# A product of constants ahead of each attention step's transposes in a one-core decoder kernel

## The chip, the cores and the metric

The kernel runs on one core of a Trainium2 chip. The metric is the device time of one execution, in microseconds (us). A profiled execution has a span (first to last instruction) that is a little shorter than its time.

## What is computed

The reference is one inference step of a decoder trunk of two layers, for a prompt of 512 tokens and for 8 sample tokens with the same weights. Layer 0 has differential attention heads and mLSTM heads side by side, layer 1 is a gated linear recurrence, and each layer ends in a SwiGLU channel mixer. Everything is float32. The part that matters here is the prompt attention of layer 0, for 4 heads and 4 blocks of 128 queries:

```python
s = jnp.einsum('bqhjd,bshjd->bhjqs', q_blk, kf)      # two key maps, j = 0, 1
s = s - slopes * dist.astype(jnp.float32)
s = jnp.where(dist >= 0, s, -jnp.inf)
p = jax.nn.softmax(s, axis=-1)
w = p[:, :, 0] - lam * p[:, :, 1]
return jnp.einsum('bhqs,bshv->bqhv', w, vf)
```

## The kernel before

The program is a setup, the input projection of layer 0, a "middle" (attention, mLSTM, the sample tokens' attention over the cached pages, and what is left of the adaLN modulation), then the output projection and the large matrix products of the rest. The order on every engine is written out by hand; engines meet only through semaphores.

The middle (`middle_pe` for TensorE) is a loop of 18 steps (s from 0 to 17), fully unrolled. Each step works on one attention unit (head h = s // 4, query block s % 4) at several stages of its life. On TensorE (PE) step s issues, in this order:

- `head_sums` (L2515 to L2527), in steps 4, 8, 12 and 16; `head_scores(s)` (L2501), the mLSTM scores; `pv(s-2)` (L2558), attention weights times values; `head_rows` (L2491) in every fourth step
- `block_products` (L2921): 64 small products for one block of the modulation, until the blocks run out
- `scores(s+1)` (L2539): the attention scores of the next unit
- `transposes(s-1)` (L2548): the weights of unit s-1, one to four tiles of 128x128, in steps 1 to 16, so 16 calls and 40 transposes in all
- `block_turn` (L2937): one product that turns the block of the step before
- then, by step: `query_rows` (L2567, steps 0 to 5), the sample tokens' work (L2577 to L2638) and `square_sums` (L2651)

PSUM is used as a ring of four buffers of two banks (`ps(g)`, group g in buffer g % 4). Every use has a number fixed by `plan()`. `begin(g)` lets PE wait until the use four before it was released by the engine that reads it, and `done` announces the result. So `head_scores(s+1)` begins only when VectorE has released the scores of `scores(s+1)`, which stand four places before it.

VectorE (DVE) issues in each step: `biased(s)` (L1591: reads and releases the scores), `past_products` for a sample token (L1640, L1644) in steps 0 to 6, `maxima` (L1597), `weights(s-1)` (L1605 to L1610, the last of which writes `Wb` and raises `w_ready`), `decayed(s)` (L1622), `block_rows` (L2046: copies `block_products`' result), `block_select` (L2060: reads `block_turn`'s result), `past_sums` (L1649, L1650), and further sample work in steps 7 to 12. Each of its calls waits for the one before it. ScalarE (ACT) takes exponentials, and `unit_wT` (L1016) copies the transposes' result out of PSUM. GpSimd (POOL) loads the cache pages (L725), two for each sample token, when the page buffer was read.

`transposes(u)` writes only the first bank of its group, and `unit_wT` reads only that one:

```python
g = use[("T", u)]
begin(g)
pe.wait_ge(w_ready, u + 1)
for kb in range(u % 4 + 1):
    ins = T.transpose(ps(g)[:, 0, kb * P:(kb + 1) * P], Wb[u % 2][:, kb * P:(kb + 1) * P], ident)
done(ins)
```

`ident` and the columns from `C_SEL` are both parts of the tile `cn`, which is loaded once with constants.

Of the kernel before, what the change touches and what calls it, by code (L numbers as in the profile page):

```python
# [69 lines left out]
C_ID, C_ADA, C_MASK, C_DIST, C_SEL, C_COMB, C_SLOPE, C_DROW = 0, 128, 168, 296, 808, 1832, 1896, 1897  # L70
# [158 lines left out]
def trunk(nc, a, o):  # L229
# [34 lines left out]
    with ExitStack() as ctx:  # L264
        def sb(name, shape, dt=F32):
            return ctx.enter_context(nc.sbuf_tensor(name, shape, dt))
# [11 lines left out]
        cn = sb("cn", [P, C_END])  # L278
# [21 lines left out]
        ident = cn[:, C_ID:C_ID + P]  # L300
# [177 lines left out]
        def ps(g):  # L478
            return psum[g % NGRP]
# [1960 lines left out]
        def middle_pe(pe, begin, done, block_products, block_turn):  # L2440
            T = nc.tensor
# [9 lines left out]
            for tb in range(4):  # L2451
                g = use[("kv", tb)]
# [9 lines left out]
            for key, first in (("stokA", 0), ("stokB", 8)):  # L2462
                g = use[key]
# [4 lines left out]
            for tb in range(4):  # L2468
                g = use[("bkv", tb)]
# [7 lines left out]
            g = use["acol"]  # L2477
# [4 lines left out]
            g = use["gs"]  # L2482
# [60 lines left out]
            def transposes(u):  # L2543
                g = use[("T", u)]
                begin(g)
                pe.wait_ge(w_ready, u + 1)
                for kb in range(u % 4 + 1):
                    ins = T.transpose(ps(g)[:, 0, kb * P:(kb + 1) * P], Wb[u % 2][:, kb * P:(kb + 1) * P], ident)  # L2548
                done(ins)
# [115 lines left out]
            for s_ in range(STEPS):  # L2665
# [14 lines left out]
                if 1 <= s_ < 17:  # L2680
                    transposes(s_ - 1)
# [23 lines left out]
            for i, t in enumerate(MIXED):  # L2705
                g = use[("rb", t)]
# [3 lines left out]
                if t == "S":  # L2710
                    for u in range(8):
                        h, j = u % 4, u // 4
                        ins = T.matmul(ps(g)[:, 0, 8 * u:8 * u + 8], cn[:, C_SEL + j * P:C_SEL + (j + 1) * P], R4[:, h, P:P + 8],
                                       start=True, stop=True)
# [3 lines left out]
                for q in range(4):  # L2718
                    b = 2 * q + j
                    ins = T.matmul(ps(g)[:, q // 2, (q % 2) * P:(q % 2 + 1) * P], cn[:, C_SEL + b * P:C_SEL + (b + 1) * P], R4[:, h, 0:P],  # L2720
                                   start=True, stop=True)
# [324 lines left out]
```

## Time and profile before

| | us |
|---|---|
| median of 3 runs | 1548.38 |
| lowest and highest | 1545.55 and 1753.03 |
| the profiled execution: time | 1548.51 |
| the profiled execution: span | 1546.9 |
| PE busy | 1419.4 (92%) |
| DVE busy | 785.6 (51%) |
| ACT busy | 532.5 (34%) |
| mean granted clock of PE | 0.955 |

The clock is given as a share of full speed: 1.0 is 2.4 GHz and 0.5 is 1.2 GHz. A float32 product shows as more than one MATMUL record (a 512-column product as two), a transpose as one. Busy shares are means over stages of different kinds. Times of single instructions are read from the timeline, where a row's start and the start of the next row tell what the first one costs in a row of work.

### The profile page before, as it was taken

How to read it: one execution, taken by the hardware profiler on the slowest of the kernel's cores; microseconds unless marked ns; L12 is line 12 of the kernel's file. 1: busy time of each engine (PE TensorE's matmuls, PEld its weight loads, DVE VectorE, ACT ScalarE, POOL GpSimd, SP SyncE). 2: the span in 40 equal slices, each digit the busy share in tenths (PEclk: the TensorE clock that was granted, in tenths of full speed). 3: DMA queues.
4: the chain of work that ended last, by engine and by line, in shares of the span. 5: the costliest groups of instructions: out<-in, count | busy, mean ns of one | idle time of the engine just before them, and what ended most of it. 6: DMA issues, size and time to landing. Idle time of an engine off the chain costs nothing.

```text
span 1546.9 us, 29445 instructions
## 1 busy us (share of the span) xinstructions
PE 1419.4 (92%) x12244; PEld 1354.5 (88%) x12244; DVE 785.6 (51%) x1181; ACT 532.5 (34%) x759; POOL 321.6 (21%) x303
## 2 busy tenths in 40 slices
PE   4999967879797999999999989988989999999996
PEld 4899956656597999999999979987989999999995
DVE  4523256763466633333324679887574333333356
ACT  1211142332423333112222346884433321222224
POOL 2000031111116500000001626534543000000054
PEclk8999988978898999999999999998999999999998
DMA  9632287756632132243322402211613224422211
GB/s 320 197 98 56 83 292 268 236 188 205 209 109 83 55 82 67 83 113 107 86 71 76 137 23 87 96 52 54 167 32 109 65 58 115 129 84 65 75 38 56
DMA packets 213504, 175.07 MB, mean 113 GB/s; under 512 B 9079, under 2 KB 183932, under 8 KB 213252
## 3 DMA queue, kind: packets, MB, share of 16 engines
q1 hardware_dynamic: 208448, 160.13, 33.7%
q0 software_dynamic: 4800, 13.23, 2.7%
q8 instruction: 81, 1.33, 0.4%
q14 instruction: 35, 0.29, 0.1%
q10 hardware_dynamic: 140, 0.09, 0.0%
HBM read 167.87 MB, written 5.63 MB: 112 GB/s over the span
## 4 chain that ended last, share of the span: by engine, by line
PE 53%; DVE 11%; ACT 3%; issue 2%; POOL 0%; DVEq 0%; ACTq 0%; POOLq 0%
PE ps L2747 44%; PE ps L2776 4%; PE ps L2756 4%; DVE gn L2196 2%; DVE wlo L1982 1%; DVE UL L2203 1%; DVE xc L2314 1%; ACT whi L1173 1%; DVE rstd L2169 1%; DVE tv L2161 0%; DVE xc L2349 0%; ACT xT L1247 0%; DVE xc L2348 0%; DVE xT L2146 0%; DVE xT L2164 0%
## 5 line engine op out<-in xcount | busy, mean ns | idle before, releaser
L2747 PE MATMUL ps<-UH,whi 128*128 128x260 f32 x1840 | 371.5, 283 | 11.2 <-DVE wlo L1982 10.8
L2747 PE MATMUL ps<-UH,wlo 128*128 128x260 f32 x1840 | 371.4, 284 | 0.0
L2747 PE MATMUL ps<-UL,whi 128*128 128x260 f32 x1840 | 370.8, 283 | 0.0
L1173 ACT ACTIVATE whi<-raw 128x2048 fp32r<-128x2048 f32 (+3 forms) x104 | 178.0, 1712 | 440.8 <-PE ps L2747 388.3
L2747 PEld LDWEIGHTS ps<-UH,whi 128*128 128x128 f32 x1840 | 284.2, 189 | 13.0 <-DVE wlo L1982 9.7
L2747 PEld LDWEIGHTS ps<-UH,wlo 128*128 128x128 f32 x1840 | 284.4, 189 | 0.0
L2747 PEld LDWEIGHTS ps<-UL,whi 128*128 128x128 f32 x1840 | 283.4, 189 | 0.0
L1982 DVE TENSOR_TENSOR wlo<-raw,whi 128x2048 fp32r<-128x2048 f32 (+3 forms) x104 | 224.1, 2155 | 77.8 <-ACT whi L1173 77.2
L2250 DVE TENSOR_TENSOR hb<-ps,silb 128x520 f32<-128x520 f32 x44 | 30.8, 699 | 268.0 <-PE ps L2747 247.9
L825 POOL COPY accS<-xT 128x520 f32<-128x520 f32 x4 | 2.5, 626 | 620.0 <-DVE xT L2128 620.0
L2747 PE MATMUL ps<-HH,whi 128*128 128x260 f32 x484 | 97.4, 283 | 0.0
L2747 PE MATMUL ps<-HH,wlo 128*128 128x260 f32 x484 | 97.1, 282 | 0.0
L2747 PE MATMUL ps<-HL,whi 128*128 128x260 f32 x484 | 97.1, 282 | 0.0
L2747 PEld LDWEIGHTS ps<-HH,whi 128*128 128x128 f32 x484 | 74.6, 189 | 0.0
L2747 PEld LDWEIGHTS ps<-HL,whi 128*128 128x128 f32 x484 | 74.5, 188 | 0.0
L2747 PEld LDWEIGHTS ps<-HH,wlo 128*128 128x128 f32 x484 | 74.2, 188 | 0.0
L2125 DVE TENSOR_TENSOR stmp<-ps,modT 128x8 f32<-128x8 f32 x36 | 6.0, 167 | 133.1 <-PE ps L2747 116.8
L2921 PE MATMUL ps<-raw,cF 128*32 128x128 f32 x1536 | 57.9, 314 | 16.5 <-DMA raw<-in_w_ada 10.1
L2921 PEld LDWEIGHTS ps<-raw,cF 128*32 128x32 f32 x1536 | 49.2, 128 | 25.7 <-DMA raw<-in_w_ada 8.5
L1320 ACT ACTIVATE silb<-ps 128x520 f32<-128x520 f32 x44 | 26.7, 606 | 127.1 <-PE ps L2747 109.3
L857 POOL TENSOR_TENSOR xT<-xT,mu 128x256 f32<-128x256 f32 x64 | 47.5, 743 | 50.9 <-ACT mu L1221 46.5
L725 POOL DMA_DIRECT2D page<-in_cache_k x16 | 8.9, 559 | 213.7 <-PE ps L2455 181.4
(509 smaller groups left out, 2577.0 us busy)
## 6 DMA issues: line engine op xcount, KB each, us to landing
raw<-in_w_ada SPq DMA_DIRECT2D x96, 512.0 KB, 6.2
raw<-in_w_ffn_in SPq DMA_DIRECT2D x88, 512.0 KB, 5.0
raw<-in_w_in_even SPq DMA_DIRECT2D x24, 512.0 KB, 4.7
raw<-in_w_ffn_out SPq DMA_DIRECT2D x32, 384.0 KB, 4.0
raw<-in_w_ffn_out SPq DMA_DIRECT2D x32, 320.0 KB, 3.4
raw<-in_w_in_odd SPq DMA_DIRECT2D x20, 512.0 KB, 4.6
raw<-in_w_out_odd SPq DMA_DIRECT2D x16, 320.0 KB, 3.6
page<-in_cache_k POOLq DMA_DIRECT2D x16, 256.0 KB, 4.5
```

What stands on the lines that cost most here:

```text
L857: pool.tensor_tensor(x, x, mu[:, hf, 0:HALF], ALU.subtract).then_inc(d_ready, 1)
L1173: ins = nc.scalar.activation(whi[w % 2][:, 0:f], raw[c % NRAW][:, 0:f], ACT.Identity)
L1320: ins = nc.scalar.activation(silb[c % 2][:], pT(g), ACT.Silu)
L1982: ins = v.tensor_tensor(wl_[:, 0:f], raw[c % NRAW][:, 0:f], wh[:, 0:f].bitcast(F32), ALU.subtract)
L2169: v.reciprocal(rstd[:, hf], tv[:, hf]).then_inc(rstd_ready, 1)
L2196: v.scalar_tensor_tensor(gn[:, t], xT[:, t, hf, 0:HALF], gain, rstd[:, hf, 0:HALF], ALU.mult, ALU.mult).then_inc(n_ready, 1)
L2203: v.scalar_tensor_tensor(UL[:, t, hf, 0:HALF], gn[:, t], B9[:, r + 1, t, 0:1], UH[:, t, hf, 0:HALF].bitcast(F32), ALU.add, ALU.subtract).t ...
L2250: v.tensor_tensor(hb[c % 2][:], pT(g), silb[c % 2][:], ALU.mult).then_inc(h_ready, 1)
L2747: ins = T.matmul(ps(g)[:, hf, 0:HT], wt(k, m), x[:, k, hf], start=(k == 0 and wt is wh and x is xh), stop=(k == s.k - 1 and wt is wl_))
L2756: ins = T.matmul(ps(g)[:, hf, 0:HT], wt(k, m), xt[:, k, hf], start=(k == 0 and wt is wh and xt is xh), stop=(k == s.k - 1 and wt is wl_), ...
L2776: ins = T.matmul(ps(g)[:, hf, 0:HT], w(k, m), x[:, k, hf], start=(i == 0 and w is wh and x is xh), stop=(i == s.k - 1 and w is wl_))
L2921: ins = T.matmul(ps(g)[32 * j:32 * j + 32, 0, 0:P], cF[:, 4 * e + k], raw[gc % NRAW][:, w0:w0 + P], start=(e == 0 and k == 0), stop=(e == ...
```

## The change

`transposes(u)` gets one more product. It multiplies the identity with 512 columns of constants (`cn` from `C_SEL`) and writes the second bank of the transposes' own group. It stands behind `begin(g)` and ahead of the wait for `w_ready`. Nothing reads its result; nothing is removed.

```diff
             def transposes(u):
                 g = use[("T", u)]
                 begin(g)
+                T.matmul(ps(g)[:, 1], ident, cn[:, C_SEL:C_SEL + 512], start=True, stop=True)
                 pe.wait_ge(w_ready, u + 1)
                 for kb in range(u % 4 + 1):
                     ins = T.transpose(ps(g)[:, 0, kb * P:(kb + 1) * P], Wb[u % 2][:, kb * P:(kb + 1) * P], ident)
```

## Rows read from the trace of the kernel before

**Rows 1.** Busy time by stage: us, each engine's busy us, PE clock, DMA share, GB/s

```profile
235.00:440.00 205.00, 165.07 (x1747) 124.22 (x1746) 125.33 (x283) 70.52 (x186) 30.99 (x44) 0.85 0.66 218
440.00:1546.00 1106.00, 1055.39 (x8510) 1039.38 (x8508) 567.49 (x739) 404.58 (x510) 264.50 (x205) 0.98 0.28 80
```

**Rows 2.** PE's waits from 235 to 440 us: total us, times, longest

```profile
PE ps L2501 <- DVE Sb L1591: 9.1, 6, 2.4
PE ps L2548 <- DVE Wb L1610: 5.5, 1, 5.5
PE ps L2617 <- DMA page<-in_cache_v: 5.2, 2, 3.3
...
PE ps L2605 <- DVE Sb L1591: 0.3, 1, 0.3
```

**Rows 3.** VectorE's waits from 235 to 440 us: its wait for block_turn

```profile
DVE modT L2060 <- PE ps L2937: 14.7, 17, 1.9
```

**Rows 4.** PE's timeline, step 2 into step 3: start, us, instructions, [idle before, releaser]

```profile
251.09 0.44 PE L2548 MATMUL ps<-cn,Wb 128*128 128x128 f32 x2
251.36 0.31 PE L2937 MATMUL ps<-cn,modrow 128*128 128x36 f32 x2
251.50 1.58 PE L2567 MATMUL ps<-cn,smp 128*128 128x128 f32 x12
254.99 0.49 PE L2501 MATMUL ps<-proj 64*128 64x128 f32 x2 [1.90 <-DVE Sb L1591]
```

**Rows 5.** VectorE's timeline in the same stretch

```profile
251.78 0.20 DVE L2060 TENSOR_TENSOR modT<-ps,bT 128x36 f32<-128x36 f32 x1 [1.25 <-PE ps L2937]
...
252.46 1.22 DVE L1650 TENSOR_REDUCE Sc<-page 128x16 f32<-128x1024 f32 x1
253.72 1.22 DVE L1591 SCALAR_TENSOR_TENSOR Sb<-cn,ps 128x1024 f32<-128x1024 f32 x1
```

**Rows 6.** PE's timeline: products of 512 float32 columns and the rows behind them

```profile
220.04 1.12 PE L2491 MATMUL ps<-rowc,cn 128*128 128x512 f32 x2
221.10 0.49 PE L2539 MATMUL ps<-proj 64*128 64x128 f32 x4
...
346.65 2.08 PE L2491 MATMUL ps<-rowc,cn 128*128 128x512 f32 x2 [3.23 <-ACT R L1052]
348.66 3.63 PE L2921 MATMUL ps<-raw,cF 128*32 128x128 f32 x64
...
353.17 1.96 PE L2638 MATMUL ps<-stok 128*128 128x512 f32 x4
355.06 1.06 PE L2617 MATMUL ps<-page,wTs 128*32 128x512 f32 x8
```

**Rows 7.** PE's timeline at the transposes of unit 0, in step 1

```profile
240.59 0.45 PE L2548 MATMUL ps<-cn,Wb 128*128 128x128 f32 x1 [5.50 <-DVE Wb L1610]
```

**Rows 8.** VectorE's timeline in step 1

```profile
237.94 0.42 DVE L1644 TENSOR_TENSOR ctmp<-Cs,ps 128x256 f32<-128x256 f32 x1
...
240.09 0.35 DVE L1610 SCALAR_TENSOR_TENSOR Wb<-Sb,st 128x128 f32<-128x128 f32 x1
```

**Rows 9.** PE's timeline at the end of step 15

```profile
403.33 1.92 PE L2617 MATMUL ps<-page,wTs 128*32 128x512 f32 x4 [1.84 <-DMA page<-in_cache_v]
408.57 1.92 PE L2617 MATMUL ps<-page,wTs 128*32 128x512 f32 x4 [3.31 <-DMA page<-in_cache_v]
```

**Rows 10.** GpSimd's timeline: the first of the four page loads behind those waits

```profile
397.21 0.55 POOL L725 DMA_DIRECT2D page<-in_cache_v  x1 [7.52 <-issue]
```

**Rows 11.** The transposes, all 40: duration in ns, least, median, most

```profile
L2548 PE MATMUL ps<-cn,Wb x40: 272/273/446, 240.6 to 421.6; 128*128 128x128 f32 x40
```

**Rows 12.** Groups by line, from 235 to 430 us: busy us, mean ns

```profile
L2921 PE MATMUL ps<-raw,cF 128*32 128x128 f32 x960 | 39.1, 331 | 6.4 <-ACT R L1052 3.5 <-ACT pvrow L1061 1.7 <-DVE proj L1770 1.1
```

**Rows 13.** PE's timeline: the same 64 products at full clock

```profile
312.11 1.95 PE L2921 MATMUL ps<-raw,cF 128*32 128x128 f32 x64
```

**Rows 14.** Busy time in two short stretches, columns as in rows 1

```profile
210.00:215.00 5.00, 5.00 (x49) 4.21 (x42) 0.68 (x3) 0.87 (x2) 0.00 (x0) 0.50 1.03 410
215.00:220.00 5.00, 4.90 (x43) 4.03 (x41) 2.59 (x5) 2.76 (x4) 4.38 (x9) 0.94 1.05 400
```

## The prediction, made before the changed kernel was run

> **What bounds the kernel.** I read the busy time by stage first. From 440 us on PE is busy for 1055 of 1106 us at a clock of 0.98, and nothing of the change lies there: a delay in the middle simply pushes this stage back [rows 1]. The middle, 235 to 440 us, is another matter. PE is busy for 165 of 205 us, VectorE for 125, and the clock is only 0.85 [rows 1]. So neither engine fills the stage; the question is which chain of waits paces a step.
>
> The waits answer that. PE waits mostly at the first product of a step, for VectorE's L1591, which releases the scores' buffer: six rows of this kind, 11 times, 16 us, of which the first and the last stand in the group [rows 2]. VectorE in turn waits in all 17 steps for L2937, PE's `block_turn` [rows 3]. The timeline of one step puts the two together. PE does the transposes at 251.09, `block_turn` at 251.36, the query rows at 251.50, and then stands idle until 254.99 [rows 4]. VectorE has been idle for 1.25 us when `block_turn` lets L2060 start at 251.78; `past_sums` and L1591 follow without a gap, and when L1591 ends at 254.94, PE starts [rows 4, 5]. The loop that paces a step is therefore: scores, transposes, `block_turn` on PE; L2060, the sample work, L1591 on VectorE; first product of the next step on PE. The idle time at its end is not slack for anything ahead of `block_turn`. The new product stands ahead of `block_turn`.
>
> **What the change adds.** Sixteen products of 512 float32 columns with a 128x128 weight. There is no such product at this place in the trace, but there are others of the same size. Two of L2638 take from 353.17 to 355.06, so 0.94 us each; one of L2491 takes from 220.04 to 221.10, so 1.06 us; at half clock one takes from 346.65 to 348.66, so 2.01 us [rows 6]. Is the clock low where the new ones stand? The 40 transposes right behind them have a median of 273 ns and a least of 272, and only one in the whole stage was clearly longer, 446 ns, that of unit 0 [rows 7, 11]. The 64 block products ahead of them have warmed the clock by then. So the price is 0.94 to 1.06 us; I take the middle, 1.0.
>
> **Where it is covered.** Unit 0: PE waits 5.5 us for `Wb` [rows 7]. The product can't start at once, since `begin` of this group waits for its fourth predecessor, the query rows that L1644 releases at 238.36. From there to the end of L1610 at 240.44 there are 2.1 us, and the product fits [rows 8]. This one is free; without that cover it would cost its 1.0 us.
>
> Unit 14, in step 15: behind its transposes PE waits 5.2 us for cache pages [rows 2, 9]. Their loads were issued from 397.21 on, ahead of this product, so their landing doesn't move with it [rows 10]. Free again. The pages move only with what delays the loads themselves, which is the other steps' cost.
>
> The other fourteen are not covered. In the steps where PE idles for L1591, VectorE's chain starts at `block_turn`, which comes 1.0 us later. In the steps without such a wait PE is simply the engine that works. Waits for ACT's copies at L2491 or L2921 hang on VectorE's `maxima`, which come behind the same L1591. Fourteen times 1.0 is **14 us** (13.2 to 14.8 from the two prices).
>
> Nothing else is added. The second bank has no reader, the group number is the old one, no semaphore is raised and no DMA is issued. SP's weight loads wait for the block products, which come ahead of the new product in their step and are delayed by earlier steps only. ACT's `unit_wT` has idle time ahead of it, and `pv` needs its copy one step later. What is late next is the chain to L1591 and, through it, all later steps.
>
> **What the clock may give back.** The middle loses time to the clock. 205 us at a mean of 0.85 means that 61.5 us were at half clock (205 x 0.15 x 2) [rows 1]. With PE busy 0.81 of the stage some 50 us of work ran there, half of which is loss: about 25 us. One part can be measured directly: the 15 sets of block products took 39.1 us, where 15 at full clock are 29.3, so 9.8 us were lost in them alone [rows 12, 13]. By the timeline there are nine such stretches, each behind an idle time of PE: the 5.5 us of unit 0 [rows 7], the pages [rows 9], and short waits of some 1.5 to 3.5 us such as that at 346.65 [rows 6]. That is 2.8 us a stretch.
>
> Does a product ahead of the transposes keep the clock up? It runs 2 to 4 us before the idle time starts, and the idle time stays as long as before, since both ends of it shift together. Only for unit 0 does it cut the idle stretch itself. I credit 2 us for that one and for luck in steps like that at 251 us, and nothing for the others; the bounds are nothing and the whole 25 us.
>
> Here a rule of the Trainium skill speaks for more. TensorE: Matmul & The Clock Gate, Part 4: PE-mode transpose, says that transposes do not count as activity for the clock gate; then the new product would be nearly the only thing that counts between the scores and the wait, and the sum would turn to a gain if most of the 25 us came back. The trace speaks against it: from 210 to 215 us the clock was 0.50, and from 215 to 220 us, when PE worked on transposes only (token rows of the sample, keys and values), it rose and was 0.94 on average [rows 14]. So here the transposes are no gap for the gate, and I keep my small credit.
>
> **The sum.** +14.0 - 2.0 = **+12 us**. The profiled execution took 1548.5 us, with a span of 1546.9; it would become 1560.5 and 1558.9. It lies 0.1 us from the median of 1548.38, which would become **1560.4**.
>
> **The rivals.**
>
> *Forecast: the product lies in series, the clock changes little.* For it: 17 of 17 waits at L2060 are for PE [rows 3]. With the two prices and a credit of 0 to 6 us: +7 to +15 us, 1555 to 1563. Chance 0.70.
>
> *The clock stays up (ends on the other side).* At each of the nine stretches the extra activity would save 2.8 us. The point that decides is five stretches: with five saved the change is at zero, with all nine it is -25 + 14 = -11 us, so 1537. For it: the clock does fall behind short waits of 1.5 to 2 us, so it must be close to staying up. Against it: the drops come behind idle stretches that the product doesn't touch, such as the page waits [rows 9] and the 3.23 us at L2491 [rows 6]. Five saved or more has a chance of 0.10, with three or four saved (+3 to +6 us, 1551 to 1554) another 0.06.
>
> The Trainium skill's section named above is the rule that would bring this about; the rows given there lower its chance.
>
> *The waits swallow the product.* If PE's 11 waits for L1591 [rows 2] were slack, those steps would cost nothing and only three of the fourteen would count: +3 us, 1551.4. For it: busy shares of 0.81 and 0.61 leave room on both engines [rows 1]. Against it: VectorE's own wait ahead of L2060 in every step [rows 3]; for this rival L1591's time must not depend on `block_turn`. Chance 0.08.
>
> *Half clock under the product.* If the shift of the steps puts the products into slow stretches, each costs 2.01 us: +28 us, 1576.5. Against it: the one slow transpose of 40 [rows 11]. A part of it (a few products at half clock, or two more slow stretches) gives +17 to +22 us. Chance 0.06.
>
> **Range and chances.** The range goes from 1547 to 1567 us: from the forecast down over the swallowed product and the clock's partial gain, and up to 14 x 1.06 plus one or two more slow stretches. Left out are five stretches saved or more (0.10) and most of the half-clock rival (0.05). A measurement of this kernel can tell about 2% from no change, which is 31 us. All cases but the far end of the last lie inside: within 2% has a chance of 0.97, slower by more 0.02, faster by more 0.01.
>
> **What the profile after would show.** 32 new MATMUL records of 128x512 at L2546, about 1.0 us for each pair up to the first transpose, at full clock. The stage that lasted from 235 to 440 us ends 12 us later, and the time from there to the end is unchanged. VectorE's wait at L2060 grows by about 1 us in fourteen steps (14.7 to some 28 us in total), while PE's waits for L1591 stay near 16 us. PE's wait for `Wb` at unit 0 shrinks by the product. The mean clock of the stage stays near 0.85 and the block products near 39 us. I would be wrong on the path if the waits for L1591 shrink by the product's time, wrong on the clock if the block products fall towards 29 us or the nine slow stretches become fewer than six, and wrong on the price if a pair of records is far from 1.0 us.

## The result, and the profile after

| | before | changed |
|---|---|---|
| median (12 runs of each) | 1547.82 us | 1552.89 us |
| lowest | 1542.6 us | 1546.43 us |
| ratio | | 1.0035, 95% interval 1.002 to 1.005 |
| the profiled execution's span | 1546.9 us | 1552.4 us |

The change makes the kernel slower by 0.35%, 5.1 us by the medians. I had forecast 12 us. The direction and the range (1547 to 1567) held, the size did not: it is less than half. This is under the 2% that I called measurable; with twelve runs of each kernel the interval nevertheless lies clear of 1.

The busy time by stage, columns as in [rows 1], for the changed kernel; the first row covers the same 205 us as the first of [rows 1]:

```profile
235.00:440.00 205.00, 169.87 (x1741) 123.34 (x1742) 120.14 (x273) 68.36 (x182) 31.06 (x44) 0.89 0.65 216
...
443.00:1552.00 1109.00, 1057.54 (x8531) 1041.52 (x8529) 570.13 (x743) 405.86 (x512) 264.65 (x205) 0.98 0.28 80
```

The last stage has the clock it had; the difference lies in the middle. There the clock went from 0.85 to 0.89. These are the last long row of products of the middle (L2720, now L2721, 40 records), first in the kernel before, then in the changed one:

```profile
432.92 6.34 PE L2720 MATMUL ps<-R,cn 128*128 128x128 f32 x40
```

```profile
438.50 6.34 PE L2721 MATMUL ps<-R,cn 128*128 128x128 f32 x40
```

That is 5.6 us later, and the span is 5.5 us longer: from this row to the end both take the same time, 1114.0 and 1113.9 us. Single profiled executions differ even where the programs are the same: PE's first product row of step 1 (L2501) already stands at 230.38 us here and at 231.43 before, 1.05 us earlier, although nothing was added ahead of it.

PE's timeline, the step that answers to [rows 4], and VectorE's, which answers to [rows 5]:

```profile
249.78 1.13 PE L2546 MATMUL ps<-cn 128*128 128x512 f32 x2
250.74 0.38 PE L2549 MATMUL ps<-cn,Wb 128*128 128x128 f32 x2
250.96 0.31 PE L2938 MATMUL ps<-cn,modrow 128*128 128x36 f32 x2
251.10 1.58 PE L2568 MATMUL ps<-cn,smp 128*128 128x128 f32 x12
254.59 0.48 PE L2501 MATMUL ps<-proj 64*128 64x128 f32 x2 [1.91 <-DVE Sb L1591]
```

```profile
251.38 0.20 DVE L2060 TENSOR_TENSOR modT<-ps,bT 128x36 f32<-128x36 f32 x1 [2.16 <-PE ps L2938]
```

PE's idle time before L2501 is 1.91 us where it was 1.90 [rows 4]: the wait swallowed nothing. VectorE's wait for `block_turn` in this step is 2.16 us where it was 1.25 [rows 5]. Over the stage, VectorE's and PE's waits (total, times, longest):

```profile
DVE modT L2060 <- PE ps L2938: 27.8, 17, 2.8
```

```profile
PE ps L2501 <- DVE Sb L1591: 9.1, 6, 2.4
...
PE ps L2546 <- DVE ctmp L1644: 3.2, 1, 3.2
PE ps L2618 <- DMA page<-in_cache_v: 2.3, 1, 2.3
```

The first rose from 14.7 us [rows 3] by 13.1: read wait by wait, 11.7 us of that belong to the fourteen steps that the prediction held to be uncovered, 1.35 to step 15 and nothing to unit 0. The second is 9.1 as before [rows 2]. The third is new and is unit 0: PE waits in `begin` for L1644, then does the product, then waits 0.8 us more for `Wb`. The last was 5.2 us [rows 2].

The cost in series is best read in a step with four tiles, before and now:

```profile
275.09 0.66 PE L2548 MATMUL ps<-cn,Wb 128*128 128x128 f32 x4
275.59 0.31 PE L2937 MATMUL ps<-cn,modrow 128*128 128x36 f32 x2
```

```profile
275.55 1.12 PE L2546 MATMUL ps<-cn 128*128 128x512 f32 x2
276.51 0.60 PE L2549 MATMUL ps<-cn,Wb 128*128 128x128 f32 x4
276.95 0.31 PE L2938 MATMUL ps<-cn,modrow 128*128 128x36 f32 x2
```

The product occupies 0.96 us up to the first transpose, but the transposes behind it take 0.44 us, where they took 0.50 (275.09 to 275.59). I read this as a start latency that now hides behind the product; no run separates it. Net 0.90 us, in fourteen steps 12.6. So 7.5 us of the 12.6 do not show in the time.

### The profile page after: what moved, and what is told of

The parts are those of the page before. It is cut to its first block, busy times and chain, and to the rows that moved or that the text cites. A ratio compares the mean times of both kernels' runs of the same rounds, so it can differ in the third digit from the quotient of the medians.

```text
span 1552.4 us, 29493 instructions
## 1 busy us (share of the span) xinstructions
PE 1428.2 (92%) x12276; PEld 1357.4 (87%) x12276; DVE 785.9 (51%) x1181; ACT 532.5 (34%) x759; POOL 321.9 (21%) x303
## 4 chain that ended last, share of the span: by engine, by line
PE 53%; DVE 11%; ACT 3%; issue 2%; POOL 0%; DVEq 0%; ACTq 0%; POOLq 0%
PE ps L2748 44%; PE ps L2777 4%; PE ps L2757 4%; DVE gn L2196 2%; DVE wlo L1982 1%; DVE UL L2203 1%; DVE xc L2314 1%; ACT whi L1173 1%; DVE rstd L2169 1%; DVE tv L2161 0%; DVE xc L2349 0%; ACT xT L1247 0%; DVE xc L2348 0%; DVE xT L2146 0%; DVE xT L2164 0%
## 5 line engine op out<-in xcount | busy, mean ns | idle before, releaser
L2748 PEld LDWEIGHTS ps<-UH,whi 128*128 128x128 f32 x1840 | 284.2, 189 | 13.1 <-DVE wlo L1982 9.7
```

The source lines that it names most:

```text
L2748: ins = T.matmul(ps(g)[:, hf, 0:HT], wt(k, m), x[:, k, hf], start=(k == 0 and wt is wh and x is xh), stop=(k == s.k - 1 and wt is wl_))
```

## Experiments

Each kernel was timed beside runs of the kernel before on the same chip. "Series cost" below is fourteen times what a trace shows between the first added product and `block_turn` in the four-tile step, less the 0.50 us of before.

**Little streaming, same time.** The question is whether the missing 7.5 us depend on what the product does.

```diff
-                T.matmul(ps(g)[:, 1], ident, cn[:, C_SEL:C_SEL + 512], start=True, stop=True)
+                for _ in range(4):
+                    T.matmul(ps(g)[:, 1, 0:2], ident, cn[:, C_SEL:C_SEL + 2], start=True, stop=True)
```

> The one product of 512 columns is replaced by four products of 2 columns each (in the trace of before, eight records of such 2-column products at L2627 last 1.03 us), so PE is held up about as long, but the array streams hardly anything. Theory A (the product costs about 0.9 us in fourteen steps, 12.7 us, and its streaming gave some 6 us back by keeping the clock up): the thin form loses the gift, so it ends 12 to 14 us above before and the clock of the middle stays near 0.85. Rival B (the clock changed in the changed kernel only because the steps were shifted in time, whatever was put in): 4 to 7 us above before, like the changed kernel. Rival C (the product is partly covered by waits and costs less than it seems): also 4 to 7 us, with PE's waits for L1591 shorter than 16 us.

Measured: 1560.66 us against 1546.85, ratio 1.0095 (1.0077 to 1.0114), 13.8 us slower. PE's timeline of the four-tile step:

```profile
278.08 1.05 PE L2547 MATMUL ps<-cn 128*128 128x2 f32 x8
279.00 0.64 PE L2550 MATMUL ps<-cn,Wb 128*128 128x128 f32 x4
279.47 0.31 PE L2939 MATMUL ps<-cn,modrow 128*128 128x36 f32 x2
```

Its cost in series is 0.89 us, as that of the wide product, and 14 x 0.89 = 12.5. The time grew by this and 1 us more, and the clock of the middle is the old one:

```profile
235.00:440.00 205.00, 175.34 (x1872) 132.45 (x1872) 115.04 (x262) 65.93 (x177) 32.07 (x46) 0.85 0.64 214
```

So the steps are delayed by as much per product as in the changed kernel, and hardly anything comes back. Theory A stands, B and C fall: with the same cost in series, the form that streams 512 columns is 8.7 us faster (13.8 - 5.1) than the form that streams 2. That 12.5 and 13.8 lie so close is partly chance: in this trace the page wait at the end of step 15 takes up 5.5 us of the delay, and slow stretches add to it.

**Twice the product.** One more line of the same kind ahead of the wait.

```diff
+                T.matmul(ps(g)[:, 1], ident, cn[:, C_SEL:C_SEL + 512], start=True, stop=True)
                 T.matmul(ps(g)[:, 1], ident, cn[:, C_SEL:C_SEL + 512], start=True, stop=True)
```

> Two products instead of one ahead of each wait. A second one costs 0.86 us or a little more in each of fourteen steps and is partly covered for unit 0 no more. Theory A: +24 us of product time less a gift of the clock of 6 to 12 us, so 13 to 20 us above before and a clock of the middle of 0.90 or more. Rival B: +25 us less or plus chance, 20 to 28 us above before, clock of the middle 0.85 to 0.88. Rival C: the second product is covered as the first would be, 8 to 12 us above before.

Measured: 1560.93 us against 1546.85, ratio 1.0101 (1.0081 to 1.012), 14.1 us slower. The trace gives 1.76 us in series, 24.6 for fourteen, so 10.5 us do not show; the clock of the middle is 0.92. The time and the clock are those of theory A. But not all of the 10.5 us came from the clock. The page wait of step 15, 5.2 us before [rows 2], is gone:

```profile
422.12 1.07 PE L2619 MATMUL ps<-page,wTs 128*32 128x512 f32 x8
```

The second product costs 12 us and the time grew by 9.0 (14.1 - 5.1); how the other 3 divide between the clock and this wait is not separated.

**Half the product.** 256 columns instead of 512.

```diff
-                T.matmul(ps(g)[:, 1], ident, cn[:, C_SEL:C_SEL + 512], start=True, stop=True)
+                T.matmul(ps(g)[:, 1, 0:256], ident, cn[:, C_SEL:C_SEL + 256], start=True, stop=True)
```

> The changed kernel's sixteen products with 256 columns instead of 512. The cost in series falls from 0.9 to about 0.48 us in each of fourteen steps, 6.7 us. If the clock's gift grows with what is streamed (about half of the 8 us that the thin form shows to be missing): 2 to 4 us above before. If any wide product gives the whole gift: at or 1 us below before. If the gift comes from nothing that is streamed: 6 to 8 us above.

Measured: 1548.87 us against 1547.06, ratio 1.0018 (1.0006 to 1.003), 1.8 us slower, with 0.47 us in series, 6.6 for fourteen. 4.8 us do not show, at a clock of 0.88 in the middle. The expectation of a gift that grows with the columns gave 2 to 4 us: the ratio (2.8 us) lies in it, the medians just below. The interval (0.9 to 4.6 us) keeps out the other two expectations.

The four forms can be compared ahead of the page wait. The table takes thirteen products, those between `block_turn` of step 1 and `block_turn` of step 14, in one profiled execution of each kernel, against the kernel before.

| form, clock of the middle | thirteen in series, us | step 14 later by, us | missing, us |
|---|---|---|---|
| 4 x 2 columns, 0.85 | 11.6 | 11.1 | 0.5 |
| 256 columns, 0.88 | 6.1 | 2.6 | 3.5 |
| 512 columns, 0.89 | 11.7 | 8.0 | 3.7 |
| 2 x 512 columns, 0.92 | 22.9 | 18.1 | 4.8 |

The wide forms give something back here and the thin one next to nothing. Between the three wide ones the differences are small for single executions.

**Behind instead of ahead.** The same sixteen products at the end of each step.

```diff
-                T.matmul(ps(g)[:, 1], ident, cn[:, C_SEL:C_SEL + 512], start=True, stop=True)
...
+                if 1 <= s_ < 17:
+                    filler(s_)          # the same product, into the bank of unit s_ - 1
             square_sums(3)
```

> The same sixteen products, each at the end of its step, behind block_turn and all else, just ahead of the wait for L1591. Theory of the path (what stands ahead of block_turn delays the loop, what stands behind it falls into PE's idle time): covered in the steps where PE idles there by 1 us or more (2 to 6, 8, 9 and 12), partly in 1, 10 and 13, exposed in 7, 11, 14 and 16: 4 to 6 us of product time, less what the clock gives back: 2 us below to 5 us above before. Rival C (the waits swallow the product wherever it stands): the same time as the changed kernel, 5 us above before, and no difference in VectorE's wait at L2060 (28 us in both).

Measured: 1549.25 us against 1546.85, ratio 1.002 (1.0009 to 1.0031), 2.4 us slower. The path theory holds. VectorE's wait at L2060 is 14.1 us, about what it was, and PE's for L1591 at L2501 fell from 9.1 us, since the products now stand in it:

```profile
PE ps L2501 <- DVE Sb L1591: 4.2, 5, 1.4
```

```profile
DVE modT L2060 <- PE ps L2944: 14.1, 17, 1.8
```

From 250 to 400 us the clock is 0.95, where it is 0.91 in the changed kernel and 0.87 before: the same products do more for it when they stand next to the idle time. So the 2.4 us are what is left of the exposed products after the clock's gift; how large each of the two is was not measured.

**Products in eight gaps.** Twelve products at the ends of steps 2 to 6, 8, 9 and 12, none elsewhere.

```diff
-                T.matmul(ps(g)[:, 1], ident, cn[:, C_SEL:C_SEL + 512], start=True, stop=True)
...
+            FILL = {2: 2, 3: 1, 4: 1, 5: 1, 6: 1, 8: 3, 9: 2, 12: 1}
...
+                if s_ in FILL:
+                    filler(s_, FILL[s_])
             square_sums(3)
```

> Products of the same kind only at the ends of steps 2 to 6, 8, 9 and 12, sized to PE's idle time there (2, 1, 1, 1, 1, 3, 2, 1 of them). The path theory has all twelve in idle time: nothing lost. If streaming in the idle time keeps the clock up (theory A), three to five of the nine slow stretches go and the time falls 5 to 12 us below before, with a clock of the middle of 0.90 or more. If the clock does not care (rival B): within 2 us of before, clock near 0.85.

Measured: 1546.81 us against 1546.85, ratio 1.0 (0.9987 to 1.0013), no change, although the clock from 250 to 400 us is 0.94. At first sight the clock does not matter. The timeline shows that I had placed two of the gaps wrongly:

```profile
316.33 1.02 PE L2596 MATMUL ps<-cn,smp 128*8 128x128 f32 x4 [3.52 <-DVE Sb L1591]
317.14 5.33 PE L2667 MATMUL ps<-cn 128*128 128x512 f32 x6
...
370.04 1.89 PE L2617 MATMUL ps<-page,wTs 128*32 128x512 f32 x8 [1.53 <-DVE Sb L1591]
371.86 1.95 PE L2667 MATMUL ps<-cn 128*128 128x512 f32 x2
```

In steps 8 and 12 the wait for L1591 is met by the step's own last call, so the products came behind the wait, on the path and mostly at half clock: 5.3 and 1.9 us. These 7.2 us can have hidden what was gained. No run moved only these two; the next one moves them and fills more gaps as well.

**Products in all gaps.** Now each stands directly ahead of the wait that it is to fill, in a bank that nobody reads. The diff is against the kernel before.

```diff
+            def stream(key, n=1):
+
+                g = use[key]
+                for _ in range(n):
+                    T.matmul(ps(g)[:, 1], ident, cn[:, C_SEL:C_SEL + 512], start=True, stop=True)
+
+            AFTER_PV = {11: 3, 12: 1, 14: 1, 15: 2}
+            AT_END = {2: 2, 3: 1, 4: 1, 5: 1, 6: 1, 9: 2}
...
+                if s_ == 7:
+                    stream(("PV", 5))            # behind head_rows
+                if s_ == 1:
+                    stream(("mS", 0, 1), 4)      # ahead of the transposes of unit 0
...
+                    stream(("T", 7), 3)          # step 8, ahead of state_values
+                if s_ == 12:
+                    stream(("T", 11))            # ahead of past_values
+                if s_ == 15:
+                    stream(("T", 14), 2)         # the same, and 3 between the two page waits
```

> Products of 512 columns in every idle time of PE in the middle, placed just ahead of the wait that ends it and sized to it: 4 ahead of the transposes of unit 0, 2 at the end of step 2, 1 each at the ends of 3, 4, 5 and 6, 3 ahead of the state values in step 8, 2 at the end of 9, 3 ahead of the wait in step 11, 1 and 1 in step 12, 1 in 7, 1 in 14, and 2, 2 and 3 around the page waits of step 15. None ahead of the transposes otherwise. If what the clock costs lies on the path (my 25 us), all nine slow stretches go and the time falls 12 to 20 us below before. If most of it is hidden (VectorE's work sets the pace as soon as PE is fast, as in the gap experiment before this one, where the clock rose and the time did not move), 2 to 7 us below before, with new waits of PE for L1610 and L1622.

Measured: 1530.84 us against 1547.06, ratio 0.9906 (0.9885 to 0.9926), 16.2 us faster. It beats both kernels. Step 8 again:

```profile
311.38 2.84 PE L2667 MATMUL ps<-cn 128*128 128x512 f32 x6
314.96 0.60 PE L2596 MATMUL ps<-cn,smp 128*8 128x128 f32 x4 [0.74 <-DVE Sb L1591]
315.49 0.92 PE L2501 MATMUL ps<-proj 64*128 64x128 f32 x4
316.34 1.16 PE L2558 MATMUL ps<-wTb,vtok 128*128 128x128 f32 x8
```

and the stage and its block products:

```profile
235.00:440.00 205.00, 186.47 (x1954) 136.97 (x1953) 136.68 (x307) 74.99 (x191) 35.91 (x48) 0.99 0.66 219
```

```profile
L2944 PE MATMUL ps<-raw,cF 128*32 128x128 f32 x960 | 29.3, 274 | 2.1 <-ACT R L1052 0.9 <-ACT pvrow L1061 0.9 <-DVE proj L1770 0.3
```

The clock is 0.99 and the block products take 29.3 us, as I had worked out for full clock, where they took 39.1 [rows 12]. Waits for L1622 rose (5 times, 3.9 us at the transposes), so a part of what the clock gives goes into waits for VectorE; of my estimate of 25 us this kernel got 16.

**The same places, little streaming.** Each product of 512 columns replaced by four of 2 columns.

```diff
-                for _ in range(n):
-                    T.matmul(ps(g)[:, 1], ident, cn[:, C_SEL:C_SEL + 512], start=True, stop=True)
+                for _ in range(4 * n):
+                    T.matmul(ps(g)[:, 1, 0:2], ident, cn[:, C_SEL:C_SEL + 2], start=True, stop=True)
```

> The kernel with products in all gaps again, with each product of 512 columns replaced by four of 2 columns, which hold PE about as long but stream almost nothing. If the 16 us came from the clock through what is streamed: the gain is gone, within 3 us of before (0 to 3 above, as some of the thin products end behind the wait they stand in), clock of the middle 0.85 to 0.87. If they came from something else that the placing does: 12 to 17 us below before, as with the wide ones.

Measured: 1550.81 us against 1547.84, ratio 1.0018 (1.0008 to 1.0028), 3.0 us slower; clock of the middle 0.87. Step 8:

```profile
314.08 3.42 PE L2667 MATMUL ps<-cn 128*128 128x2 f32 x24
317.67 1.01 PE L2596 MATMUL ps<-cn,smp 128*8 128x128 f32 x4 [0.17 <-DVE Sb L1591]
318.61 1.65 PE L2501 MATMUL ps<-proj 64*128 64x128 f32 x4
```

PE has hardly been idle, and still L2501 takes 1.65 us, the time at half clock, against 0.92 behind the wide products. So the 16 us come from the clock, and filling the same gaps with 2-column products did not keep it up.

**The change on top of full clock.** The product ahead of the transposes added to the kernel with all gaps filled, for the fourteen units other than 0 and 14.

```diff
                 begin(g)
+                if u not in (0, 14):
+                    T.matmul(ps(g)[:, 1], ident, cn[:, C_SEL:C_SEL + 512], start=True, stop=True)
                 pe.wait_ge(w_ready, u + 1)
```

> The kernel with products in all gaps, plus the change's own product ahead of the transposes of the fourteen units other than 0 and 14. The clock is at 0.99 already in the middle, so nothing is left to give back and the cost in series shows alone. If it is 0.9 us in each of fourteen steps: 12 to 13 us above the kernel with the gaps filled, so 3 to 5 us below before. If part of it is covered by waits (those for L1622, 5 times there): 8 to 11 us above it.

Measured: 1544.86 us against 1547.84, ratio 0.9981 (0.9969 to 0.9992), 3.0 us faster than before. That is 13.2 us above the kernel without these products when each is taken against its own runs of before by the medians, and 11.6 us by the ratios. The last long row of the middle moved from 414.61 to 426.90, 12.3 us. With the clock at 0.99 in both there is next to nothing to give back, and the price shows nearly in full (14 x 0.90 = 12.6). Step by step it is cleanest from `block_turn` of step 2 to that of step 14: twelve products, 10.0 us, 0.84 each. The rest of the 12.3 us is 0.7 us that the execution was late in step 1 already and 1.7 us in step 2, where beside the product the block products were slow (3.31 us against 1.96). The product of unit 15 was offset by what was left of the page wait.

**The two covered ones alone.** The change's product only for units 0 and 14.

```diff
+                if u in (0, 14):
+                    T.matmul(ps(g)[:, 1], ident, cn[:, C_SEL:C_SEL + 512], start=True, stop=True)
```

> The changed kernel's product kept only for units 0 and 14, the two that the prediction held to be covered, by the wait for Wb and by the page waits. Covered and without effect on the clock: within 1 us of before. If a product costs its 0.9 us wherever it stands: 2 us above. If the one of unit 0 saves the slow stretch behind it: 2 to 3 us below.

Measured: 1548.41 us against 1547.06, ratio 1.0006 (0.9992 to 1.0021). The interval goes from 1.2 us below to 3.2 us above before; it excludes the 2 to 3 us of gain at unit 0, but it can't tell "free" from "0.9 us each". The trace can. At unit 0 `block_turn` starts 0.65 us behind the end of L1610 in both kernels (242.28 and 241.63 here, 241.09 and 240.44 before), so the product adds nothing. At unit 14 it does delay `block_turn`, which is 2.0 us later than before instead of the 1.1 us of the steps ahead of it, and the page wait takes that up: the next two `block_turn` and the last long row are 1.0 us later.

```profile
401.02 1.12 PE L2547 MATMUL ps<-cn 128*128 128x512 f32 x2
...
402.31 0.31 PE L2939 MATMUL ps<-cn,modrow 128*128 128x36 f32 x2
...
409.45 1.92 PE L2619 MATMUL ps<-page,wTs 128*32 128x512 f32 x4 [4.28 <-DMA page<-in_cache_v]
```

Of this 1.0 us, 0.8 stood there already at the block products of step 1 (233.12 against 232.28), ahead of the first added product.

## Why the prediction was right and wrong

**What bounds the middle: right.** The loop through `block_turn`, L2060 and L1591 was shown three ways. VectorE's wait at L2060 grew by 13.1 us while PE's wait at L2501 stayed at 9.1; the same products behind `block_turn` left the first at 14.1 and cut the second to 4.2; and with the clock held at full speed fourteen of them cost 11.6 to 13.2 us.

**The price: too high by a tenth.** I took 1.0 us from products of the same size. The nearest rows gave 0.94 and 1.06; the product takes 0.96, and the transposes behind it got 0.06 shorter. Fourteen times 0.90 is 12.6, not 14.0.

**Covered at units 0 and 14: right in the traces, but the page wait covers more.** For unit 0 the waits of 3.2 and 0.8 us around the product stand where 5.5 us stood [rows 7], and it did start only when L1644 was through. The slow stretch behind it stayed: `query_rows` at 240.36 still took 2.91 us. The 2 us that I credited mostly to this place were not earned there. For unit 14 the page wait covered more than the product. This is the end of step 15 and the products ahead of it:

```profile
404.74 3.16 PE L2922 MATMUL ps<-raw,cF 128*32 128x128 f32 x64 [1.99 <-ACT R L1052]
407.83 1.55 PE L2546 MATMUL ps<-cn 128*128 128x512 f32 x2
...
413.98 1.05 PE L2618 MATMUL ps<-page,wTs 128*32 128x512 f32 x4 [2.28 <-DMA page<-in_cache_v]
```

The block products were slow there (3.16 us, against 1.96 for the same row at 398.04 before) and the product took 1.38 us. With these 2.5 us and what came from the steps before, `block_turn` of step 15 stands 9.2 us later (409.54 against 400.31), but the products on the second page stand only 5.4 us later (413.98 against 408.57 [rows 9]). The wait took up 3.8 us: the 2.5, and 1.3 us of what the other steps had cost. I had written that the pages move with what delays their loads; the first load was issued 6.2 us later (403.38 against 397.21 [rows 10]), so this sentence too was wrong by about 1 us. In the thin form the wait took up 5.5 us.

**What the clock gives back: the step that failed.** I wrote that the product runs 2 to 4 us before the idle time, that the idle time stays as long, and I credited 2 us. The idle time did stay as long, but the conclusion was false. Against the thin form, which costs the same in series, the wide one is 8.7 us faster. In the profiled execution the rows that got faster, less those that got slower, add up to about 4.8 us (the slow ones ahead of the page wait left out, since it covers them). So the term was 5 to 9 us and not 2. That the time still fell inside the range is due to the range's low end, which reached down over a partial gain of the clock, and not to this term. That execution can be added up from the start: 12.6 us of product, 0.5 us of new waits for L1622, less 4.8 us by the clock, less 1.3 us in the page wait, less 1.2 us by which it was ahead at the end of unit 0, is 5.8 us, and 5.6 were measured. The 7.5 us by the medians (12.6 - 5.1) are thus mostly the clock, but not only.

The block products, which I had named as the sign, show less than half of it: 39.1 us before [rows 12] and now

```profile
L2922 PE MATMUL ps<-raw,cF 128*32 128x128 f32 x960 | 37.0, 319 | 6.4 <-ACT R L1052 3.5 <-ACT pvrow L1061 1.7 <-DVE proj L1770 1.2
```

The slow stretches that had followed the waits at 277 and 364 us are gone. Around the second of them PE's timeline had

```profile
366.34 3.33 PE L2921 MATMUL ps<-raw,cF 128*32 128x128 f32 x64 [1.73 <-ACT pvrow L1061]
...
373.43 1.94 PE L2617 MATMUL ps<-page,wTs 128*32 128x512 f32 x8 [1.53 <-DVE Sb L1591]
375.30 1.65 PE L2501 MATMUL ps<-proj 64*128 64x128 f32 x4
```

and now has

```profile
373.07 1.96 PE L2922 MATMUL ps<-raw,cF 128*32 128x128 f32 x64 [1.73 <-ACT pvrow L1061]
...
379.70 1.06 PE L2618 MATMUL ps<-page,wTs 128*32 128x512 f32 x8 [1.53 <-DVE Sb L1591]
380.69 0.99 PE L2501 MATMUL ps<-proj 64*128 64x128 f32 x4
```

The waits are as long as they were (1.73 and 1.53 us), and the rows are at full clock. In this execution the clock outlasted such waits more often than before. It did not in every case: the stretches behind the 3.5 us wait of step 8, the 2.4 us wait of step 9 and the 3.23 us wait of step 11 remained.

**The clock rival was undervalued in its middle.** I gave 0.10 to five stretches saved or more and 0.06 to three or four. The result lies in the latter's 3 to 6 us: 4.8 to 8.7 us are two to three stretches of 2.8 us. The argument that I used against it, the clock that rose during transposes [rows 14], is a right reading, but it says nothing of how many stretches the product saves. I took from the Trainium skill's rule (TensorE: Matmul & The Clock Gate, Part 4: PE-mode transpose) that the product would be nearly all that counts in its stretch. That does not follow in steps 1 to 5, where `block_turn` and the query rows, 1.58 us of products [rows 4], stand there as well. Whether transposes count was not tried in any run. What the thin forms show is narrower: 24 records of two-column products in 3.4 us, with PE's time nearly full, did not keep the clock, and six records of 512 columns in 2.8 us did.

**The other rivals.** "The waits swallow the product" is refuted by the 9.1 us that stayed. "Half clock under the product" occurred in part in two places: unit 0 (its records last 1.31 us instead of 1.12), where it is covered, and unit 14 (1.55 us), where it is covered too.

A spread belongs to this. Over the twelve runs of the changed kernel the mean clock of a run goes from 0.959 to 0.968 and the time from 1556.4 to 1546.4 us, one with the other (correlation -0.96). The profiled one, at 1554.06 us and 0.959, is at the slow end. Which stretches are slow differs from trace to trace, so a single profiled pair is a sample: the comparisons above that rest on medians are firmer than the account of single stretches. What decides for one given wait whether the clock falls stays open.

## What to carry to other kernels

Before calling idle time slack, ask what starts the chain that ends it: work put ahead of the instruction that starts the other engine's chain is paid nearly in full (0.84 to 0.90 us for each product here), the same work behind it falls in part into the idle time. With the clock's gift taken off, sixteen products cost 5.1 us ahead and 2.4 us behind. In this kernel products that are only there to keep the clock up, placed directly ahead of each wait and sized to it, were worth 16 us, and the same kind of product in the wrong place cost 5. Check in the timeline which instruction meets the wait: products that stood one call too late took 7.2 us on the path.

When the clock rises and less time is lost than was added, do not put the whole difference down to the clock: look also at the waits for DMA further down, which can take up a delay (3.8 us here).

## What the runs showed of the hardware

How long PE was occupied did not alone decide its clock: with the same gaps filled, the granted clock of the middle was 0.99 with 512-column products and 0.87 with two-column ones, and 0.85 with nothing. A wait of 1.73 us was followed by half clock in the kernel before (366.34 us) and by full clock in the changed one (373.07 us); with the 3.5 us wait of step 8 filled but for 0.74 us the clock held. A 512-column float32 product ahead of a transpose costs 0.90 us net, a second one behind it 0.86, and a 256-column one 0.47.
